# A SwiGLU FFN multiplied as 2x2 blocks with seven block products for eight, in a decoder step on one core

## The chip, the core and the metric

The kernel runs on one core of one Trainium2 chip. A core has TensorE (matmuls, PE in the rows; PEld is its weight load, which overlaps PE), VectorE (DVE), ScalarE (ACT), GpSimd (POOL) and SyncE (SP, which here issues nearly all DMAs). The engines run each their own instruction list and meet at semaphores. The metric is the time of one execution of the program on the device, in microseconds; less is better.

## The reference

One layer of a decoder: RMSNorm, one combined projection, sparse attention (compressed, selected and window branches) beside a pooling group, an output projection with a second norm and the residual, and then the part that the change touches, for 1024 prompt rows and 64 sample rows (1088 rows in all) of width 1024, with 2816 columns in the hidden layer:

```python
D_FF = -(-8 * D_MODEL // (3 * 256)) * 256
...
def ffn_block(x, g_pre, g_post, w_gate, w_up, w_down):
    h = rms_norm(x, g_pre)
    f = (jax.nn.silu(h @ w_gate) * (h @ w_up)) @ w_down
    return x + rms_norm(f, g_post)
```

All values are fp32. The kernel writes each fp32 operand as a high and a low part in fp16 and forms every product from three fp16 matmuls (high-high, high-low, low-high), summed in PSUM.

## The kernel before

Up to about 715 us of the span the program loads, projects and attends. Then come four stages.

**Output projection and second norm.** Nine row tiles t (eight of 128 rows, the last of 64). TensorE forms `project(t)` (L1667: 8 slices of the contraction, 2 halves of 512 columns, 3 matmuls each, so 48) and then `turn(t-1)` (L1678: 8 transposes of the normed rows of the tile before). GpSimd splits the mix operand of a tile ahead of it (`slot_mix`, L1636 and L1640); ScalarE makes the sums of squares (`norms`), VectorE the residual rows x1 (`residual`), the normed rows (`normed`) and, from PSUM, the transposed operand h2 (`save`). ScalarE and VectorE split h2 into its parts (`high`, `low`). The residual rows x1 of all tiles stay in SBUF.

**Gate and up.** For each of 22 tiles f of 128 hidden columns TensorE takes three chunks of rows (384, 384, 320) and for each chunk 24 matmuls with w_gate and 24 with w_up (L1700). Two 512 KB DMAs bring the raw weights of a tile, ScalarE casts the high part (L1791), VectorE makes the low part (L1930). Out of PSUM, ScalarE applies silu (L1819), VectorE multiplies (L1965), ScalarE casts (L1821) and GpSimd makes the low part (L1650).

**Down.** For each of 8 output tiles k TensorE takes the same three chunks, 66 matmuls each over the 22 hidden tiles (L1700 too); the weights (1408 KB each) are split as before (L1795, L1934), ScalarE copies the results out (L1844).

**End.** The last output tile's chunks, transposes back (L1736), the norm's squares (L1864), the scaling (L1994), the adding of x1 (L1653 on GpSimd, L1999 on VectorE) and the stores.

The order on every engine is the order in which the code is written; no scheduler moves anything. Semaphores carry the waits. The free regions of SBUF are laid out by hand in one `arena`.

## Time and profile before

| | us |
|---|---|
| median of 3 runs | 1589.15 (1588.97 to 1590.52) |
| profiled execution, span | 1590.2 |
| TensorE busy | 1446.0 (91%) |
| matmuls of gate and up, first to last | 827.70 to 1317.16 |
| matmuls of down with the transposes among them | 1319.97 to 1567.76 |
| VectorE, ScalarE, GpSimd busy | 709.0, 552.8, 407.0 |

The page shows one execution; times are counted from the start of its span. A row of the chain says when a group of instructions starts and how long it takes, with its engine, line and count. Rows of lines give the busy time of a group, the mean duration of one instruction in ns (for a matmul this holds its whole way through the array, and matmuls overlap), and the idle time before it. The granted clock of TensorE is 1.00 at 2.4 GHz and 0.50 at 1.2 GHz.

### The profile page before, as it was taken

To read this page: it belongs to the slowest core of one execution; us is meant where nothing else is said; L and a number is where in the kernel's file an instruction comes from. 1 tells how busy PE (TensorE), PEld (TensorE's weight loads), DVE (VectorE), ACT (ScalarE), POOL (GpSimd) and SP (SyncE) were. 2 spreads that over 40 slices of the span, in tenths; PEclk is the share of its full clock that TensorE was granted. 3 is DMA by queue.
4 is the path that set the end of the run, shared out by engine and by line. 5 is a ranking of instruction groups with operands and counts; after the bars stand their busy time and mean duration, and the time that the engine had idled before them with its cause. 6 is when DMAs were issued, how large, how long until landed. Compare 5 with 4: busy or idle time off the path is not lost.

```text
span 1590.2 us, 25581 instructions
## 1 busy us (share of the span) xinstructions
PE 1446.0 (91%) x10276; PEld 855.7 (54%) x10276; DVE 709.0 (45%) x1176; ACT 552.8 (35%) x1203; POOL 407.0 (26%) x459
## 2 busy tenths in 40 slices
PE   5498897887899889979979999999999999999996
PEld 3244443544444446644446666666666665666664
DVE  5799995784788536665551111111111120100103
ACT  5233324655677456653341222212222121111103
POOL 1344433785667501013201111111111110000004
PEclk9699998977999899989989999999999999999998
DMA  9666643000000256752111111111111121121102
GB/s 379 217 216 202 208 153 115 1 1 1 1 2 1 107 239 279 310 161 62 53 46 40 53 53 34 45 53 53 53 33 46 53 73 37 47 63 36 36 14 113
DMA packets 93475, 146.59 MB, mean 92 GB/s; under 512 B 3691, under 2 KB 74831, under 8 KB 91143
## 3 DMA queue, kind: packets, MB, share of 16 engines
q1 hardware_dynamic: 81823, 78.43, 15.7%
q0 software_dynamic: 11520, 67.11, 11.7%
q8 instruction: 50, 0.82, 0.2%
q14 instruction: 26, 0.21, 0.0%
q10 hardware_dynamic: 56, 0.01, 0.0%
...
## 4 chain that ended last, share of the span: by engine, by line
PE 61%; ACT 1%; DVE 1%; DMA 1%; issue 1%; POOL 0%; DVEq 0%; POOLq 0%; ACTq 0%
PE psum L1700 46%; PE psum L1667 6%; PE psum L1218 2%; PE psum L1230 2%; PE psum L1256 1%; PE psum L1278 1%; DMA arena<-in_cache_kv_sel,sel_idx 1%; PE psum L807 1%; PE psum L1736 0%; ACT arena L1352 0%; PE psum L1678 0%; DVE arena L1994 0%; ACT arena L1864 0%; PE psum L1285 0%; PE psum L1234 0%
## 5 line engine op out<-in xcount | busy, mean ns | idle before, releaser
L1700 PE MATMUL psum<-arena 128*128 128x384 f16 (+1 forms) x4752 | 734.8, 318 | 5.4 <-POOL arena L1650 2.8
L1700 PEld LDWEIGHTS psum<-arena 128*128 128x128 f16 x4752 | 466.2, 98 | 273.5 <-issue 10.5
L1965 DVE SCALAR_TENSOR_TENSOR arena<-psum,arena 128x384 f32<-128x384 f32 (+1 forms) x66 | 35.4, 536 | 349.1 <-ACT arena L1819 349.1
L1650 POOL TENSOR_TENSOR arena<-arena 128x384 f32 (+1 forms) x66 | 57.7, 874 | 465.2 <-ACT arena L1821 465.2
L2308 PE MATMUL psum<-arena 128*128 128x512 f16 (+1 forms) x768 | 153.2, 360 | 0.0
L1819 ACT ACTIVATE arena<-psum 128x384 f32<-128x384 f32 (+1 forms) x66 | 31.2, 473 | 338.0 <-PE psum L1700 338.0
L1128 POOL TENSOR_TENSOR arena<-arena 128x768 f32<-128x768 f32 (+3 forms) x96 | 131.3, 1382 | 5.0
L997 ACT ACTIVATE arena<-psum,arena 128x384 f32<-128x384 f32 (+3 forms) x192 | 104.7, 554 | 53.3 <-DVE arena L1041 23.0
L2075 POOL DMA_INDIRECT arena<-in_cache_kv_cmp,cmp_idx x64 | 85.3, 1332 | 140.3 <-DVE arena L2239 100.0
L2308 PEld LDWEIGHTS psum<-arena 128*128 128x128 f16 x768 | 76.1, 99 | 72.7 <-issue 4.7
L1934 DVE SCALAR_TENSOR_TENSOR arena<-arena 128x2816 f16<-128x2816 f32 x8 | 24.7, 3093 | 173.7 <-ACT arena L1795 173.7
L1667 PE MATMUL psum<-arena 128*128 128x512 f16 (+1 forms) x432 | 97.3, 387 | 4.9 <-POOL arena L1640 4.9
L941 PE MATMUL psum<-arena 128*128 128x128 f32 x528 | 90.2, 296 | 9.2 <-POOL arena L1128 9.1
L953 PE MATMUL psum<-arena 128*64 128x256 f32 x528 | 90.5, 424 | 3.6 <-DVE arena L1061 2.8
L1038 DVE TENSOR_REDUCE arena<-psum 128x2 f32<-128x768 f32 (+3 forms) x96 | 85.5, 891 | 13.4 <-PE psum L928 10.5
L941 PEld LDWEIGHTS psum<-arena 128*128 128x128 f32 x528 | 59.3, 147 | 53.5 <-issue 37.2
L928 PE MATMUL psum<-arena 64*128 64x384 f16 (+3 forms) x576 | 64.5, 333 | 23.9 <-ACT arena L997 12.5
L1653 POOL TENSOR_TENSOR arena<-arena 128x1024 f32<-128x1024 f32 x7 | 16.3, 2366 | 247.4 <-DVE arena L1994 247.4
L1844 ACT ACTIVATE arena<-psum 128x384 f32 (+3 forms) x21 | 9.9, 473 | 188.2 <-PE psum L1700 188.2
L1930 DVE SCALAR_TENSOR_TENSOR arena<-arena 128x2048 f16<-128x2048 f32 x22 | 50.4, 2293 | 52.3 <-ACT arena L1791 52.3
L2238 DVE TENSOR_TENSOR arena<-arena 128x1024 f32<-128x1024 f32 x56 | 68.3, 1220 | 12.0 <-DMA arena<-in_cache_kv_cmp,cmp_idx 11.1
L1667 PEld LDWEIGHTS psum<-arena 128*128 128x128 f16 (+1 forms) x432 | 43.4, 101 | 55.9 <-POOL arena L1640 5.1
...
## 6 DMA issues: line engine op xcount, KB each, us to landing
arena<-in_w_gate SPq DMA_DIRECT2D x22, 512.0 KB, 3.9
arena<-in_w_up SPq DMA_DIRECT2D x22, 512.0 KB, 5.1
arena<-in_w_down SPq DMA_DIRECT2D x8, 1408.0 KB, 7.0
arena<-in_x_prompt SPq DMA_DIRECT2D x16, 512.0 KB, 4.7
...
arena<-in_cache_kv_win SPq DMA_DIRECT2D x8, 512.0 KB, 3.5
out_y_prompt<-arena SPq DMA_DIRECT2D x8, 512.0 KB, 2.6
...
```

The source lines that it names most:

```text
L928: ins = pe.matmul(bank(2 * (x.n % 2) + g)[:, 0:x.nb * P], qT_half[r, NT - 1 - u.i, qp, x.j, :], kT_half[r, kp, 1 if u.kind == "sel" else 0 ...
L941: ins = pe.transpose(bank(4 + t % 2)[:, (2 * g + jj) * P:(2 * g + jj + 1) * P], u.P[:, jj, g, k * P:(k + 1) * P], ident)
L953: ins = pe.matmul(bank(u.bank)[g * HD:(g + 1) * HD, 0:2 * P], z_all[:, u.k0 + k, u.v0 + g * HD:u.v0 + (g + 1) * HD], pT[t % 3][:, g, :], s ...
L997: ins = nc.scalar.activation(u.P[:, x.jj, g, x.b0 * P:(x.b0 + x.nb) * P], bank(2 * (x.n % 2) + g)[:, 0:x.nb * P], ACT.Exp, bias=neg_m[x.n ...
L1038: ins = nc.vector.tensor_reduce(neg_m[x.n % 4], S, AX, ALU.max, negate=True)
L1128: ins = nc.gpsimd.tensor_tensor(part, part, x[:, c, :].unsqueeze(2).broadcast_to([P, G, nb * P]), ALU.mult)
L1650: nc.gpsimd.tensor_tensor(row(1), silu_out[c][:, 0:c1 - c0], row(0), ALU.subtract).then_inc(act_ready, 1)
L1667: ins = pe.matmul(bank(2 * s + h)[0:n, :], mix_slot[s][xp][:, k, 0:n], w_out[wp][:, k, 512 * h:512 * (h + 1)], start=(k == 0 and i == 0), ...
L1700: ins = pe.matmul(out[:, 0:c1 - c0], w[wp][:, k, :], x[xp][:, k, c0:c1], start=(k == 0 and i == 0), stop=(k == n_k - 1 and i == 2))
L2075: nc.gpsimd.indirect_dma_start(raw[k % RAW].rearrange("p c r -> p (c r)"), None, cmp_rows, bass.IndirectOffsetOnAxis(ap=cmp_idx[:, k:k + 1 ...
L2238: step(nc.vector.tensor_tensor(rows, rows, pos, ALU.mult))
L2308: ins = pe.matmul(dst[:, 0:n], hT[s][xp][:, k, :], w_in[wp][:, k, c0:c0 + n], start=(k == 0 and i == 0), stop=(k == KD - 1 and i == 2))
```

## The change

The FFN's three matrix products are now computed by blocks. The operand h2 is cut into 2 halves of the contraction and 2 halves of the rows (B11, B21 on the left, B12, B22 on the right, 544 rows each), the weights into 2 halves of the contraction and 2 halves of the output (A11 to A22). Seven block products take the place of eight, with sums of blocks as operands: S1 to S4 of the weights, T1 to T4 of h2 and later of the activation. A block product of gate and up has 4 slices of the contraction, 3 matmuls each, in two chunks of 272 rows: 12 matmuls for each product and chunk, 14 of those (168 matmuls) for a unit, which is one pair of hidden tiles (f, f+11) of one of the two matrices. There are 22 units, gate and up in turn. In the down product one of 28 steps s has one operand of 11 slices and two chunks: 66 matmuls of 272 columns. P1, P6, P5 and P3 of a unit add to one another in one PSUM bank for each chunk: each waits until the sum so far has been copied out. P4 adds to P7 in the same way; P2 stands alone.

What else it adds: on GpSimd the sums of h2 (`h_sums`, 4 for a pair of row tiles), of the weights (`w_sum`, 4 for a unit) and of the down weights (`d_sum`, one or two of 1408 columns for a step), and the low halves of the activation's sums (`combine_low`); on ScalarE and VectorE the splits of these sums, copies and adds of single products (`save_u`, `take`, `copy_out`, `add_out`). Row tiles of the output projection are taken in pairs (m, m+4), which lie side by side in the two halves. The rows x1 are written to DRAM as they are made and read back (`x1_dram`) in the last stage. Raw down weights come in 40 DMAs of 704 KB through a ring of 5 buffers. The diff, cut to what bears on the order and on the cost:

```diff
+        OPS = ("B11", "B21", "T1", "T4", "T3", "T2", "B22")
+        HALF, TC = 544, 272
...
+        W_OPS = ("A11", "A22", "A12", "S1", "S2", "S3", "S4")
...
+        PRODUCTS = {"P1": ("A11", "B11"), "P6": ("S2", "T2"), "P2": ("A12", "B21"), "P5": ("S1", "T1"),
+                    "P7": ("S3", "T3"), "P3": ("S4", "B22"), "P4": ("A22", "T4")}
...
+        D_ORDER = ("P1", "P2", "P6", "P5", "P7", "P4", "P3")
+        D_LOADS = {"P1": ((0, 0),), "P2": ((1, 0),), "P6": ((0, 4), (1, 4), (0, 0)), "P5": (), "P7": ((0, 0), (0, 4)), "P4": ((1, 4),),
+                   "P3": ((1, 0), (0, 0))}
...
+        PREP_AT = {s: max(s - 2, -1) for s in range(LAST)}
+        PREP_AT.update({LAST: 21, LAST + 1: 22, LAST + 2: 23, LAST + 3: 24})
...
+        ORDER = [(p, c) for p in ("P6", "P2", "P5", "P7", "P3", "NEXT", "P4") for c in range(2)]
...
+            with sp.Fori(0, KF - 1) as f:
+                sp.wait_ge(w_low, f * 14 + 14)
+                load_gu(f + 1, 0)
+                sp.wait_ge(w_low, f * 14 + 21)
+                load_gu(f + 1, 1)
...
+            for i, (s, kh, m) in enumerate(d_load):
+                if i == 2:
+                    sp.wait_ge(a_low, A0 + 4 * KF)
+                if i >= NR:
+                    sp.wait_ge(dw_low, d_load[i - NR][0] + 1)
+                sp.dma_start(d_raw[i % NR], down_v[:, kh * KF:(kh + 1) * KF, m * P:(m + 1) * P]).then_inc(dl_loaded[i % NR], 16)
...
+                pool.wait_ge(h2_ready, m * 4 + 2)
+                nc.gpsimd.tensor_tensor(b11, b12, b11, ALU.subtract).then_inc(h2_sums, 1)
+                pool.wait_ge(h2_sums, m * 4 + 1)
+                nc.gpsimd.tensor_tensor(b12, b22, b12, ALU.subtract).then_inc(h2_sums, 1)
+                pool.wait_ge(h2_sums, m * 4 + 2)
+                nc.gpsimd.tensor_tensor(b22, b22, b11, ALU.subtract).then_inc(h2_sums, 1)
+                pool.wait_ge(h2_sums, m * 4 + 3)
...
+            with pool.Fori(0, 2) as m:
+                slot_mix(m + 1, 1)
+                h_sums(m)
+                slot_mix(m + 2, 0)
+            slot_mix(3, 1)
+            h_sums(2)
+            slot_mix(NT, 0)
...
+                pool.wait_ge(w_low, u * 7 + 2)
+                nc.gpsimd.tensor_tensor(raw_q["S1"], raw_q["A21"], raw_q["A22"], ALU.add).then_inc(w_sums, 1)
+                pool.wait_ge(w_sums, u * 4 + 1)
+                nc.gpsimd.tensor_tensor(raw_q["S3"], raw_q["A11"], raw_q["A21"], ALU.subtract).then_inc(w_sums, 1)
+                pool.wait_ge(w_sums, u * 4 + 2)
...
+                if name in ("P6", "P7", "P3"):
+                    for i in range(d_first[s], d_first[s + 1]):
+                        pool.wait_ge(dl_loaded[i % NR], 16 * (i // NR + 2))
+                n = d_sums[0]
+                if name == "P6":
+                    nc.gpsimd.tensor_tensor(s1_f[m], raws[0], raws[1], ALU.add).then_inc(dw_sums, 1)
+                    pool.wait_ge(dw_sums, n + 1)
+                    nc.gpsimd.tensor_tensor(raws[2], s1_f[m], raws[2], ALU.subtract).then_inc(dw_sums, 1)
...
-                        ins = pe.matmul(out[:, 0:c1 - c0], w[wp][:, k, :], x[xp][:, k, c0:c1],
-                                        start=(k == 0 and i == 0), stop=(k == n_k - 1 and i == 2))
-                return ins
...
+                        ins = pe.matmul(out[:, 0:TC], w[wp][:, k, :], x[xp][:, k, c * TC:(c + 1) * TC],
+                                        start=(first and k == 0 and i == 0), stop=(k == n_k - 1 and i == 2), skip_group_check=not first)
+                ins.then_inc(done, 1)
...
+                pe.wait_ge(w_low, u * 7 + W_OPS.index(A) + 1)
+                if p == "P1":
+                    if not first:
+                        pe.wait_ge(c12_taken, u * 2 + (c - 3))
+                elif p == "P6":
+                    pe.wait_ge(s1_saved, u * 2 + (c + 1))
+                elif p == "P5":
+                    pe.wait_ge(chain_saved, saved_at(u, "P6", c))
+                elif p == "P3":
+                    pe.wait_ge(chain_saved, saved_at(u, "P5", c))
+                elif p == "P4":
+                    pe.wait_ge(c22_taken, u * 2 + (c + 1))
...
+            w_highs(0, 0, W_OPS)
             step.at(end)
             norms(NT, 0)
...
+            high_right(3)
+            high_sums(3)
...
+            act.wait_ge(p1_done, 1)
+            save_1(0, 0, 0)
+            save_u(0, 0, "P6", 0)
+            save_u(0, 0, "P5", 0)
+            silu_12(0, 0)
+            high_left(4)
+            high_right(4)
+            high_sums(4)
...
+                step.at(start + (m * 2) * 3)
+                residual(m * 2 + 2, 0, m * 16 + 32, m * 16 + 16)
+                save(m * 2 + 1, 1)
+                normed(m * 2 + 2, 0)
+                low_right(m)
+                step.at(start + (m * 2 + 1) * 3)
+                residual(m * 2 + 3, 1, m * 16 + 32, m * 16 + 16)
+                low_sums(m)
+                dve.wait_ge(h2_ready, m * 4 + 4)
+                save(m * 2 + 2, 0)
+                normed(m * 2 + 3, 1)
+                low_left(m + 1)
...
+            w_lows(0, 0, W_OPS)
+            residual(NT, 0, 16 * (NT // 2 + 1), 16 * (NT // 2))
             save(NT - 1, 1)
             normed(NT, 0)
-            low(NT - 1, 1)
+            low_right(3)
...
```

`PRODUCTS` gives for each product its weight block and its right operand; `ORDER` is the order of a unit, where NEXT is P1 of the next unit. Three places of the instruction lists follow, each before and now.

TensorE, from the last tile of the output projection into the FFN (L1667 and L1927 project, L1678 and L1938 turn, L1959 a block product):

```order
L1667 MATMUL psum<-arena 64x512 [waits x1_done,mix_ready]
L1667 MATMUL psum<-arena 64x512 x47
L1678 MATMUL psum<-arena 128x128 [waits h2_read,xn_ready]
L1678 MATMUL psum<-arena 128x128 x7
L1678 MATMUL psum<-arena 128x64 [waits h2_read,xn_ready]
L1678 MATMUL psum<-arena 128x64 x7
L1706 UNCONDITIONAL_BRANCH [waits h2_ready]
L1706 ISA
L1711 ISA [waits gu_split]
```

```order
L1927 MATMUL psum<-arena 64x512 [waits x1_done,mix_ready]
L1927 MATMUL psum<-arena 64x512 x47
L1938 MATMUL psum<-arena 128x128 [waits h2_read,xn_ready]
L1938 MATMUL psum<-arena 128x128 x7
L1959 MATMUL psum<-arena 128x272 [waits w_low,x1_done,h2_ready]
L1959 MATMUL psum<-arena 128x272 x11
L1959 MATMUL psum<-arena 128x272 [waits w_low]
L1959 MATMUL psum<-arena 128x272 x11
L1959 MATMUL psum<-arena 128x272 [waits s1_saved,w_low]
L1959 MATMUL psum<-arena 128x272 x11
L1959 MATMUL psum<-arena 128x272 [waits w_low]
L1959 MATMUL psum<-arena 128x272 x11
```

The transposes of the 64-row tile (128x64 before) no longer stand ahead of the FFN's first matmuls: P1 and P2 of the first chunk come first, then P6 with a wait for `s1_saved`, ScalarE's copy of P1.

ScalarE at the same place (L1770/L1771 and L2092/L2093 the norms, L1787 and L2117 to L2126 high parts of h2, L1791 and L2135 high parts of weights, L1819 silu, L2164 the copy of P1, L2169 of later sums):

```order
L1791 ACTIVATE arena<-arena 128x2048 [waits gu_loaded]
L1770 ACTIVATE arena<-psum 64x1024 [waits o_done]
L1771 ACTIVATE arena<-arena 64x1 [waits act_norm_step]
L1770 ACTIVATE arena<-arena 64x1024 [waits x1_done]
L1771 ACTIVATE arena<-arena 64x1 [waits act_norm_step]
L1787 ACTIVATE arena<-arena 128x8x128 [waits h2_read]
L1787 ACTIVATE arena<-arena 128x8x64 [waits h2_read]
L1791 ACTIVATE arena<-arena 128x2048 [waits gu_loaded,h2_ready]
L1819 ACT_TABLE_LOAD [waits act_ready]
L1819 ACTIVATE arena<-psum 128x384 [waits gu_done]
```

```order
L2135 ACTIVATE arena<-arena 128x512 [waits weight_loaded5]
L2135 ACTIVATE arena<-arena 128x512 x2
L2135 ACTIVATE arena<-arena 128x512 [waits w_sums] x4
L2092 ACTIVATE arena<-psum 64x1024 [waits o_done]
L2093 ACTIVATE arena<-arena 64x1 [waits act_norm_step]
L2092 ACTIVATE arena<-arena 64x1024 [waits x1_done]
L2093 ACTIVATE arena<-arena 64x1 [waits act_norm_step]
L2117 ACTIVATE arena<-arena 128x4x128 [waits h2_read]
L2125 ACTIVATE arena<-arena 128x8x128 [waits h2_sums]
L2126 ACTIVATE arena<-arena 128x8x128
L2164 ACTIVATE arena<-psum 128x272 [waits p1_done]
L2169 ACTIVATE arena<-psum 128x272 [waits prod_done] x2
```

Seven splits of the first unit's weights, four of them behind `w_sums`, now stand ahead of the norms of the last tile, and the high parts of h2's sums, behind `h2_sums`, ahead of the copy of P1.

GpSimd at the end of the output projection (L1636/L1640 and L1798/L1802 are `slot_mix`, L1815 to L1821 `h_sums`, L1838 to L1842 `w_sum`):

```order
L1636 ISA [waits o_done]
L1636 COPY arena<-arena 128x1024
L1640 TENSOR_TENSOR arena<-arena 128x1024 [waits mix_high]
L1635 REGISTER_ALU
L1636 ISA [waits o_done]
L1636 COPY arena<-arena 128x1024
L1640 TENSOR_TENSOR arena<-arena 128x1024 [waits mix_high]
L1624 REGISTER_ALU
L1624 COMPARE_AND_BRANCH
L1636 CAST arena<-arena 128x8x64 [waits o_done]
L1640 TENSOR_TENSOR arena<-arena 128x8x64 [waits mix_high]
```

```order
L1826 COMPARE_AND_BRANCH
L1798 CAST arena<-arena 128x1024 [waits o_done]
L1802 TENSOR_TENSOR arena<-arena 128x1024 [waits mix_high]
L1815 TENSOR_TENSOR arena<-arena 128x512 [waits h2_ready]
L1817 TENSOR_TENSOR arena<-arena 128x512 [waits h2_sums]
L1819 TENSOR_TENSOR arena<-arena 128x512 [waits h2_sums]
L1821 TENSOR_TENSOR arena<-arena 128x512 [waits h2_sums]
L1798 CAST arena<-arena 128x8x64 [waits o_done]
L1802 TENSOR_TENSOR arena<-arena 128x8x64 [waits mix_high]
L1838 TENSOR_TENSOR arena<-arena 128x512 [waits w_low]
L1840 TENSOR_TENSOR arena<-arena 128x512 [waits w_sums]
L1842 TENSOR_TENSOR arena<-arena 128x512 [waits w_sums]
```

Four sums of h2, the first behind `h2_ready`, now stand between the mix operands of an odd tile and of the next even tile; the same happens in each turn of the loop before these rows. The first unit's weight sums follow.

## Rows read from the trace of the kernel before

**Rows 1.** The page, busy time of each engine and share of the span.

```profile
PE 1446.0 (91%) x10276; PEld 855.7 (54%) x10276; DVE 709.0 (45%) x1176; ACT 552.8 (35%) x1203; POOL 407.0 (26%) x459
```

**Rows 2.** Chain that ended last: start us, us, engine, tile, line, count.

```profile
806.82 10.49 PE psum L1667 x48
...
827.70 489.46 PE psum L1700 x3168
...
1319.97 236.21 PE psum L1700 x1518
1556.18 2.62 PE psum L1736 x24
1558.80 8.96 PE psum L1700 x66
```

**Rows 3.** TensorE by line and shape: busy us, mean ns, idle before.

```profile
L1700 PE MATMUL psum<-arena 128*128 128x384 f16 x3168 | 524.0, 328 | 5.4 <-POOL arena L1650 2.8 <-DVE arena L1925 2.5
L1700 PE MATMUL psum<-arena 128*128 128x320 f16 x1584 | 220.1, 299 | 0.0
...
L466 PE MATMUL psum<-arena 128*128 128x64 f16 x96 | 3.5, 193 | 1.2 <-ACT arena L559 1.2
```

**Rows 4.** Timeline of TensorE in the input projection (L2308).

```profile
122.68 10.52 PE L2308 MATMUL psum<-arena 128*128 128x512 f16 x48
...
135.22 8.20 PE L2308 MATMUL psum<-arena 128*128 128x512 f16 x48
```

**Rows 5.** Timeline of the output projection, all engines.

```profile
712.02 2.87 POOL L1640 TENSOR_TENSOR arena<-arena 128x1024 f16<-128x1024 f16 x1 [0.19 <-POOL arena L1636]
...
749.96 1.04 POOL L1636 CAST arena<-arena 128x1024 f16 x1 [7.88 <-PE psum L1667]
750.49 10.52 PE L1667 MATMUL psum<-arena 128*128 128x512 f16 x48
751.18 2.13 POOL L1640 TENSOR_TENSOR arena<-arena 128x1024 f16<-128x1024 f16 x1 [0.18 <-POOL arena L1636]
...
756.23 0.75 DVE L1913 TENSOR_SCALAR arena<-arena 128x1024 f32 x1
...
795.58 1.16 POOL L1640 TENSOR_TENSOR arena<-arena 128x512 f16<-128x512 f32 x1 [0.18 <-POOL arena L1636]
```

**Rows 6.** Windows: us, PE, PEld, DVE, ACT, POOL busy, clock, DMA.

```profile
825.00:830.00 5.00, 2.47 (x10) 1.13 (x9) 2.26 (x4) 3.22 (x3) 0.00 (x0) 0.50 0.02 3
830.00:835.00 5.00, 5.00 (x23) 2.60 (x22) 1.63 (x1) 0.60 (x1) 0.00 (x0) 0.69 0.39 115
1320.00:1325.00 5.00, 5.00 (x21) 2.55 (x22) 2.69 (x1) 2.27 (x1) 0.00 (x0) 0.66 0.00 0
```

**Rows 7.** The other engines by line and shape, columns as Rows 3.

```profile
L1930 DVE SCALAR_TENSOR_TENSOR arena<-arena 128x2048 f16<-128x2048 f32 x22 | 50.4, 2293 | 52.3 <-ACT arena L1791 52.3
L1934 DVE SCALAR_TENSOR_TENSOR arena<-arena 128x2816 f16<-128x2816 f32 x8 | 24.7, 3093 | 173.7 <-ACT arena L1795 173.7
L1965 DVE SCALAR_TENSOR_TENSOR arena<-psum,arena 128x384 f32<-128x384 f32 x44 | 24.5, 558 | 219.1 <-ACT arena L1819 219.1
...
L1821 ACT ACTIVATE arena<-arena 128x384 f32 x40 | 20.9, 522 | 28.9 <-DVE arena L1965 28.9
L1795 ACT ACTIVATE arena<-arena 128x2816 f16<-128x2816 f32 x8 | 20.4, 2544 | 1.1 <-POOL arena L1650 1.1
...
L1128 POOL TENSOR_TENSOR arena<-arena 128x512 f32<-128x512 f32 x28 | 31.1, 1111 | 0.6
...
L1653 POOL TENSOR_TENSOR arena<-arena 128x1024 f32<-128x1024 f32 x7 | 16.3, 2366 | 247.4 <-DVE arena L1994 247.4
```

**Rows 8.** DMA issues: count, KB each, median us to landing.

```profile
arena<-in_w_up SPq DMA_DIRECT2D x22, 512.0 KB, 5.1
arena<-in_w_down SPq DMA_DIRECT2D x8, 1408.0 KB, 7.0
```

**Rows 9.** Timeline after the last matmul, VectorE scaling a group.

```profile
1572.65 3.67 DVE L1994 SCALAR_TENSOR_TENSOR arena<-psum,arena 128x1024 f32<-128x1024 f32 x3
```

899 lines of the change are left out of this document (660 added, 239 removed).

## The prediction

> **What bounds the kernel now.** I read the busy line of the page first: TensorE is busy for 91% of the span and no other engine for half of it [rows 1]. Then the chain of what ended last: after 806.82 it is TensorE nearly throughout, 3168 matmuls of gate and up in 489.46 us, then 236.21, 2.62 and 8.96 us for down with its transposes [rows 2]. The list by line and shape says that TensorE idled only 5.4 us before all 4752 of them [rows 3]. So the FFN stands at the array's own rate, and what counts is how many columns stream and who is late once fewer do.
>
> The rate: 48 matmuls of 512 columns take 10.52 us, of which some 0.16 is the drain of the last, so 215.8 ns each, 213.3 ns of streaming at 2.4 GHz and 2.5 more. In the row of 8.20 us the code has 24 matmuls of 512 columns and 24 of 280 (the rows of a project with two outputs); without the drain and the 24 long ones 2.86 us are left, 119.2 ns each, again 2.5 above 280 columns [rows 4]. So 272 columns cost 115.8 ns, and a product of 12 matmuls 1.39 us. The weight load is no floor: 96 matmuls of 64 columns, each with its own 128x128 load, were busy 3.5 us, 36 ns each [rows 3].
>
> The Trainium skill speaks against this size: "TensorE: Matmul & The Clock Gate", section "Back-to-back issue gap", has a stream of load and matmul pairs at about 81 ns for 128 columns, some 25 ns above streaming. By that (an estimate from the page) the new FFN would be 5544 x 22 ns = 122 us dearer than mine, and slower than before, as a rival below has it. The row of 280 columns shows no such surcharge.
>
> **The change part by part.** Arithmetic alone: before, 3168 matmuls of 384 columns at 162.5 ns and 1584 of 320 at 135.8 give 729.9 us; after, 22 x 168 + 28 x 66 = 5544 of 272 columns give 642.0. That is 87.9 us less. Where it goes I work out in four stretches of time against the profiled execution (span 1590.2; the median of the runs is 1.05 lower).
>
> *Output projection, +21.* TensorE has 11.2 us for a tile (10.4 for 48 matmuls, 0.9 for the transposes). GpSimd now does `h_sums` between the mix operands of an odd tile and the next even one. These sums wait for `low_right`, which stands on VectorE behind `normed` of the even tile. In the old trace that tile's project ended at about 749.7 (the cast at 749.96 answers to it) and its normed rows at 756.98 [rows 5]. Half a tile's low part takes 0.7 more (1024/2 elements at the 1.1 ns of L1934 [rows 7] and an access): 757.7. Four sums of 512 elements at 1.11 to 1.16 us [rows 5, 7] with 0.18 between: 763.0. Then the next mix operand, 1.04 + 0.18 + 2.13 + 0.1: 766.5. TensorE, which began the odd tile at 750.49, would want it at 761.7. It waits 4.8 to 4.9 us, and so for tiles 4, 6 and 8; behind the mix operand nothing else stands but the next one, in time. Such a gap also lowers the clock: after an idle of 2.8 us the granted clock was 0.66 over 1320 to 1325, after the one before 827.70 it was 0.50, then 0.69 over 830 to 835 [rows 3, 6]. At half the clock these cost 1.5 and 2.7 us; I take 2.1 for each gap of this size or larger. Sum 3 x (4.9 + 2.1) = 21.0; the bounds are 0 (all in time) and 3 x 9. On VectorE and ScalarE the added splits (about 3 us for a pair of tiles) lie in the 22 us that the pair takes.
>
> *From the start of the last project to the first down matmul, -43.* Before: 806.82 to 1319.97, 513.2 us [rows 2]. After, counted from the last project's start: ScalarE reaches `w_highs` at 6.3 (norms of tile 7 until 0.5, two high parts of sums, the save of tile 6 behind their low parts at 5.2, one more high part); A11 and A22 are split at 8.8 on VectorE; four sums of the weights (4 x 1.34) end at 14.2 and the seventh high part at 14.9. Only then come the norms of the last tile, though its project ended at 10.4. Start of norm to normed rows is 7.1 (749.9 to 756.98 [rows 5]): 22.0. Low part 22.7, `h_sums(3)` 28.0, two high parts of 1024 (1.04 each) 30.2, and only behind these, on ScalarE, the copy of P1: 30.6. TensorE has done P1 and P2 by 14.1, and P6 waits 16.6 us. The change lets FFN work begin before the last transposes, but the wait takes that back. Then five products, 2.7 for the low clock, 0.6 for the step from P5's copy to P3: 41.0. Transposes 41.9. The right columns of the 64-row tile (save, splits, four small sums, splits) take until 48.2, 6.3 us idle. Nine more products with the low clock and a step: 64.0. By now 16 of the 308 products are done; 292 x 1.39 = 405.8 follow, so down begins at 469.8. The old 2.8 us wait before down goes, since a first step's weights and operand are ready while P4 of the last unit runs. 469.8 - 513.2 = -43.4; were the first unit free of waits, it would be -75.
>
> That the steady units keep pace is the claim on which most rests. A unit has 19.45 us. For two units VectorE has 14 low parts of 512 elements (0.6, from L1930 and L1934), 12 takes of 272 columns (0.45, from L1965) and some 5 us more: 19 of 38.9 us; ScalarE 14 high parts (0.6), 14 copies and silus of 272 (0.4) and 7 of 544 (0.65): 19; GpSimd 8 sums (1.16) and 4 low parts (1.2): 15 [rows 7]. The chain P6, P5, P3 has four other products between, 4.2 to 5.6 us, for a copy that needs 0.6. The tightest place is the reload of the one raw weight buffer. The last weight split of an up unit stands behind two casts of the activation and ends near 19.2; the load lands about 6 us later (5.1 and the issue [rows 8]); two splits, two takes and a silu later ScalarE copies P5's first chunk at 9.9 of the next unit, where P3 wants it at 11.1. Slack about 1 us, then 2 us at the copy of P1.
>
> *Down, -16.* Before: 1319.97 to 1567.76, 247.8 [rows 2]. After: 1848 x 115.8 = 214.0 and six tiles' transposes 5.2. A step takes 7.64. Steps 8 to 11 (P6) need three raw loads each in a ring of five, and the last load of a step waits until the step before it has its low part. So the steps' weights form a serial loop: load 5.0 (between 512 KB at 5.1 and 1408 KB at 7.0, a lone one somewhat quicker [rows 8]), two GpSimd sums of 1408 elements at 3.0 (from L1128 and L1653), high part 1.36 (L1795 halved and a little), low part 1.63 (L1934), handovers 0.5: 14.7 a step. Step 8's low part is ready at 50.2 after down's start (after step 5, at 45.8), the next at 64.9, 79.6 and 94.3. TensorE wants them at 61.1, 68.7, 76.4 and then 7.64 after. It waits 3.2 and 7.1, and 2.1 for the clock: 12.4. P7 and P3 have two loads a step and come in time. VectorE with two combines a step is busy 7.2 of 7.64, and its low parts have 9 us of slack. 231.6 - 247.8 = -16.2; bounds -28 (no wait) and -5 (sums at 3.3, loads at 5.5, the later steps late too).
>
> *End, -5.* Before, 22.4 us from the last matmul to the end, in which VectorE scaled two groups of tiles, 3.67 each [rows 2, 9]. After, tiles 0 to 5 are turned among the last eight products, and one group is left: add 0.5, copy 0.6, transposes to 3.7, squares and root to 6.3, scaling 3.9, adds 2.5, store as before 4.7: 17.5. Bounds 14 and 22. x1's way through DRAM is queued while the last steps run and costs nothing; without that cover it would be 4.2 MB, some 21 us at the rate of 1408 KB in 7.0 [rows 8].
>
> Sum: 21.0 - 43.4 - 16.2 - 5.0 = -43.6, span 1546.6, time 1546.
>
> **The rivals.** *The waits are covered (0.2).* If GpSimd's sums go faster or overlap more than read here, the gaps of the output projection and of P6 close: 1546 - 21 - 12 = 1513. For it: GpSimd is busy only 407 us. Against: the order is strict, and each sum waits for the one before.
>
> *The units run longer than TensorE's share (0.11): slower than before.* The place is the reload round of the raw weight buffer above. It becomes the bound once the round passes 19.45; the change turns slower from 44/22 = 2 us over that. Casts and sums on GpSimd beside VectorE splits took 2.87 in place of 2.13 us [rows 5], a factor of 1.35; on all sums and low parts of a round (5.4 and 9 us) this is 5 us, of which idle time would take some 2. At 22.5 us a unit: 1546 + 22 x 3 = 1612. Against: both engines are idle half of the time, and a round by itself is about 15 us (load 6, sums 5.4, four splits at its ends).
> The Trainium skill, "SBUF — State Buffer", on the engine side of the ports, has VectorE and GpSimd share one pair, the loser blocked for the whole instruction; by that this factor would be larger for the f32 sums. The row of 2.87 shows some of it.
>
> *The short matmuls cost more than 115.8 ns (0.03),* by waits at every twelfth: 8 ns more each is 44 us and no gain, 1590; 16 ns more are 1635. Against: 2.5 ns at 280 as at 512 columns [rows 4]. The surcharge of the Trainium skill's section named above would come out here.
>
> *Some units stall by the 1 us slack (0.06):* ten pairs with 1 to 2 us, 1556 to 1566, still faster.
>
> **How the numbers follow.** The forecast has 0.6: 1546, its own range 1530 to 1562. The range for 8 in 10 reaches to the covered case and to the stalling units: 1508 to 1580. A change of 0.2% (3 us) is about what a measurement of this kernel can tell from none. Faster: 0.6 + 0.2 + 0.06, less a little for errors that add: 0.85. Slower: 0.12. Same: 0.03.
>
> **What would show it.** Right: 5544 matmuls with 115 to 117 ns spacing; three gaps of 4 to 6 us ahead of projects of even tiles, each after GpSimd; a gap of 15 us or more before the first P6, behind ScalarE; two waits in down at steps 10 and 11; units of 19.4 to 19.6 us. Wrong: units above 20 us, or a spacing above 120 ns, or no gaps before the FFN. The forecast fails most likely in the first unit and in GpSimd's durations.

## The result, and the profile after

The changed kernel takes 1600.9 us (median of 6 runs, 1597.5 to 1603.9) against 1590.0 for the kernel before on the same chip (6 runs): ratio 1.0065, 95% interval 1.0049 to 1.0081. It is slower by 11 us; 1546 us was forecast, and the range ended at 1580.

| stretch | before | after | change | forecast |
|---|---|---|---|---|
| to the start of the last project | 806.8 | 821.0 | +14.2 | +21.0 |
| from there to the first down matmul | 513.2 | 474.0 | -39.1 | -43.4 |
| down | 247.8 | 284.1 | **+36.3** | **-16.2** |
| end | 22.4 | 16.9 | -5.5 | -5.0 |
| span | 1590.2 | 1596.0 | +5.8 | -43.6 |

Three stretches came within 7 us. Down is off by 52 us. The table is of one profiled execution, whose span lies 3 us under the median of the six. The first down matmul stands inside a merged row and is reckoned back from its steps, so down and end are good to 0.3 us. The busy line of the page, answering to [rows 1]:

```profile
PE 1380.2 (86%) x11068; PEld 938.7 (59%) x11068; DVE 1017.4 (64%) x1623; ACT 666.0 (42%) x1491; POOL 675.7 (42%) x598
```

TensorE is busy for 66 us less, VectorE for 308 more and GpSimd for 269 more. The average does not say where that hurts. TensorE's timeline does (start, us, engine, line, count, and in brackets the idle time before and who ended it). Output projection and first unit:

```profile
765.48 12.22 PE L1927 MATMUL psum<-arena 128*128 128x512 f16 x48 [4.15 <-POOL arena L1802]
...
793.95 12.18 PE L1927 MATMUL psum<-arena 128*128 128x512 f16 x48 [4.14 <-POOL arena L1802]
...
820.99 12.23 PE L1927 MATMUL psum<-arena 128*64 128x512 f16 x48 [2.75 <-POOL arena L1802]
...
853.96 6.66 PE L1959 MATMUL psum<-arena 128*128 128x272 f16 x36 [16.93 <-ACT arena L2164]
...
870.10 9.90 PE L1959 MATMUL psum<-arena 128*128 128x272 f16 x60 [5.33 <-DVE arena L2371]
```

The three gaps ahead of even tiles are there, each behind GpSimd's mix operand, and each project after one takes 1.7 us longer than the 10.52 of the others. P6 of the first chunk waits 16.9 us for ScalarE's copy of P1 (16.6 forecast).

The steady units, one window of 40 us (columns: TensorE, its weight loads, VectorE, ScalarE, GpSimd busy with their counts, granted clock, DMA share and GB/s):

```profile
1100.00:1140.00 40.00, 39.89 (x345) 33.48 (x343) 22.58 (x35) 17.00 (x39) 17.33 (x13) 1.00 0.19 52
```

That is 116 ns for each matmul, with 0.1 us of idle; three more such windows have 344 to 347 matmuls and at most 0.3 us of idle. Now down (L2494 is VectorE's split of a weight block into its low part, L2522 the low part of a combined activation block):

```profile
1269.95 94.00 PE L1959 MATMUL psum<-arena 128*128 128x272 f16 x810 [0.34 <-ACT arena L2169]
1364.25 7.82 PE L1959 MATMUL psum<-arena 128*128 128x272 f16 x66 [0.31 <-DVE arena L2494]
1378.54 10.67 PE L1959 MATMUL psum<-arena 128*128 128x272 f16 x66 [6.47 <-DVE arena L2494]
1393.45 17.70 PE L1959 MATMUL psum<-arena 128*128 128x272 f16 x132 [4.24 <-DVE arena L2494]
1411.41 7.82 PE L1959 MATMUL psum<-arena 128*128 128x272 f16 x66 [0.26 <-DVE arena L2494]
1420.67 7.82 PE L1959 MATMUL psum<-arena 128*128 128x272 f16 x66 [1.45 <-DVE arena L2494]
1432.21 9.46 PE L1959 MATMUL psum<-arena 128*128 128x272 f16 x66 [3.72 <-DVE arena L2494]
...
1476.12 7.82 PE L1959 MATMUL psum<-arena 128*128 128x272 f16 x66 [1.45 <-DVE arena L2494]
...
1536.64 6.32 PE L1959 MATMUL psum<-arena 128*128 128x272 f16 x33 [9.51 <-DVE arena L2522]
```

Nine steps run at 7.64 us, from 1295.0 (nine steps before the end of the first row) to 1363.95. Steps 10 and 11 wait 6.5 and 4.2; the loop of P6 was forecast to make them wait 3.2 and 7.1. But then nearly every step waits for VectorE's low part: the steps start 9.27 us apart, and 11.55 where GpSimd makes the weight sums of P7 while VectorE splits the weights of steps 15 to 18. All waits of down for L2494 are 36.0 us in 14 places, and the one for the combined operand B22 (L2522) is 9.5. The longer waits also lower the clock: after 3.72 us of wait step 15 took 9.46 in place of 7.82, with a granted clock of 0.55 from 1432.3 to 1436.0; after 1.45 us step 14 took 7.82, at 1.00 from 1420.7 to 1428.0.

I call a slot what an engine does for one step, and a combination the making of one slice of a combined activation block: VectorE adds high parts (L2515) and then the low parts that GpSimd's `combine_low` has added (L2517), ScalarE takes the new high part (L2283), VectorE the new low part (L2522). One slot of 9.27 us, all engines but TensorE:

```profile
1403.27 0.78 DVE L2509 TENSOR_TENSOR arena<-psum,arena 128x272 f32<-128x272 f32 x2
...
1403.96 0.71 DVE L2515 TENSOR_TENSOR arena<-arena 128x544 f32<-128x544 f16 x1
1404.71 0.72 DVE L2517 TENSOR_TENSOR arena<-arena 128x544 f32<-128x544 f32 x1
1405.36 0.72 DVE L2515 TENSOR_TENSOR arena<-arena 128x544 f32<-128x544 f16 x1
1405.47 0.66 ACT L2283 ACTIVATE arena<-arena 128x544 f16<-128x544 f32 x1 [5.05 <-DVE arena L2517]
1405.52 1.63 POOL L1902 TENSOR_TENSOR arena<-arena 128x544 f32<-128x544 f16 x1 [5.82 <-DVE arena L2517]
1406.11 1.62 DVE L2517 TENSOR_TENSOR arena<-arena 128x544 f32<-128x544 f32 x1
1407.77 0.66 ACT L2283 ACTIVATE arena<-arena 128x544 f16<-128x544 f32 x1 [1.64 <-DVE arena L2517]
1407.81 1.22 POOL L1902 TENSOR_TENSOR arena<-arena 128x544 f32<-128x544 f16 x1 [0.66 <-DVE arena L2517]
1408.33 1.36 ACT L2265 ACTIVATE arena<-arena 128x1408 f16<-128x1408 f32 x1
1409.72 1.63 DVE L2494 SCALAR_TENSOR_TENSOR arena<-arena 128x1408 f16<-128x1408 f32 x1 [1.99 <-ACT arena L2265]
1411.27 1.35 DVE L2522 TENSOR_TENSOR arena<-arena 128x544 f16<-128x544 f32 x2
```

Two things make 6.4 us of work last 9.3. The second L2517 takes 1.62 us where the first took 0.72: GpSimd's `combine_low` had started 0.59 before it, and it ends 0.6 after that has ended. (`combine_low` is stretched too: 1.63 beside VectorE's L2515, 1.22 at 1407.81, where VectorE stands idle.) And VectorE stands idle for 1.99, since ScalarE takes the two combinations first and the weight split (L2265), which had been free to start, last. Where a weight sum of P7 falls into the slot a third thing comes on top:

```profile
1427.52 3.15 POOL L1886 TENSOR_TENSOR arena<-arena 128x1408 f32<-128x1408 f32 x1
1428.26 3.90 DVE L2494 SCALAR_TENSOR_TENSOR arena<-arena 128x1408 f16<-128x1408 f32 x1 [1.99 <-ACT arena L2265]
```

The split started 0.74 after GpSimd's weight sum and ended 1.49 after it, so it had moved hardly anything while the sum ran: 3.90 for 1.63. GpSimd's two sums for each step of P3 do the same later, ahead of the waits of 3.7 and 3.6 at steps 22 and 23 and of the 9.5 for B22:

```profile
1502.24 3.90 DVE L2494 SCALAR_TENSOR_TENSOR arena<-arena 128x1408 f16<-128x1408 f32 x1 [1.99 <-ACT arena L2265]
...
1516.73 7.02 DVE L2494 SCALAR_TENSOR_TENSOR arena<-arena 128x1408 f16<-128x1408 f32 x2 [1.99 <-ACT arena L2265]
```

### The profile page after: what moved, and what is told of

It reads as the page before. It is cut to its first block, busy times and chain, and to the rows that moved or that the text cites. A ratio compares the mean times of both kernels' runs of the same rounds, so it can differ in the third digit from the quotient of the medians.

```text
span 1596.0 us, 28892 instructions
## 1 busy us (share of the span) xinstructions
PE 1380.2 (86%) x11068; PEld 938.7 (59%) x11068; DVE 1017.4 (64%) x1623; ACT 666.0 (42%) x1491; POOL 675.7 (42%) x598
## 4 chain that ended last, share of the span: by engine, by line
PE 16%; DVE 15%; issue 12%; DMA 10%; ACT 7%; POOL 3%; DVEq 1%; SPq 1%; ACTq 0%; POOLq 0%
PE psum L1959 6%; DMA arena<-in_w_up 3%; DMA arena<-in_w_gate 3%; DVE arena L2376 3%; PE psum L1927 2%; ACT arena L2135 2%; DMA arena<-in_cache_kv_sel,sel_idx 2%; DVE arena L2418 2%; DVE arena L2494 2%; PE psum L1221 2%; ACT arena L2265 2%; PE psum L1233 2%; DVE arena L2517 1%; DVE arena L2522 1%; DVE arena L2515 1%
## 5 line engine op out<-in xcount | busy, mean ns | idle before, releaser
L1959 PE MATMUL psum<-arena 128*128 128x272 f16 x5544 | 666.7, 284 | 70.3 <-DVE arena L2494 36.0
L1959 PEld LDWEIGHTS psum<-arena 128*128 128x128 f16 x5544 | 549.2, 99 | 186.5 <-DVE arena L2494 40.1
L2376 DVE SCALAR_TENSOR_TENSOR arena<-arena 128x512 f16<-128x512 f32 x154 | 138.4, 929 | 171.4 <-ACT arena L2135 171.4
L2879 PE MATMUL psum<-arena 128*128 128x512 f16 (+1 forms) x768 | 153.0, 360 | 0.0
L2494 DVE SCALAR_TENSOR_TENSOR arena<-arena 128x1408 f16<-128x1408 f32 x28 | 64.9, 2319 | 88.5 <-ACT arena L2265 88.5
L2879 PEld LDWEIGHTS psum<-arena 128*128 128x128 f16 x768 | 76.2, 99 | 72.6 <-issue 4.3
L1927 PE MATMUL psum<-arena 128*128 128x512 f16 (+1 forms) x432 | 101.7, 398 | 16.1 <-POOL arena L1802 15.9
L2135 ACT ACTIVATE arena<-arena 128x512 f16<-128x512 f32 x154 | 89.4, 624 | 44.5 <-DMA arena<-in_w_up 28.7
L1851 POOL TENSOR_TENSOR arena<-arena 128x544 f32 (+1 forms) x44 | 60.1, 1375 | 90.5 <-ACT arena L2184 90.5
L1838 POOL TENSOR_TENSOR arena<-arena 128x512 f32<-128x512 f32 x22 | 28.7, 1306 | 162.2 <-DVE arena L2376 162.2
L944 PEld LDWEIGHTS psum<-arena 128*128 128x128 f32 x528 | 58.8, 146 | 53.1 <-issue 36.3
L1902 POOL TENSOR_TENSOR arena<-arena 128x544 f32<-128x544 f16 x33 | 46.3, 1405 | 95.0 <-DVE arena L2517 94.9
L1927 PEld LDWEIGHTS psum<-arena 128*128 128x128 f16 (+1 forms) x432 | 44.2, 103 | 71.0 <-POOL arena L1802 16.8
L1355 ACT ACTIVATE arena<-psum 128x512 f32<-128x512 f32 (+2 forms) x104 | 53.1, 558 | 59.0 <-PE psum L1221 38.6
## 6 DMA issues: line engine op xcount, KB each, us to landing
arena<-x_dram SPq DMA_DIRECT2D x2, 2048.0 KB, 10.8
```

The source lines that it names most:

```text
L944: ins = pe.transpose(bank(4 + t % 2)[:, (2 * g + jj) * P:(2 * g + jj + 1) * P], u.P[:, jj, g, k * P:(k + 1) * P], ident)
L1927: ins = pe.matmul(bank(2 * s + h)[0:n, :], mix_slot[s][xp][:, k, 0:n], w_out[wp][:, k, 512 * h:512 * (h + 1)], start=(k == 0 and i == 0), ...
L1959: ins = pe.matmul(out[:, 0:TC], w[wp][:, k, :], x[xp][:, k, c * TC:(c + 1) * TC], start=(first and k == 0 and i == 0), stop=(k == n_k - 1 ...
L2135: nc.scalar.activation(slots[w][name][0], raw_q[name], ACT.Copy, scale=WS).then_inc(w_high, 1)
L2376: nc.vector.scalar_tensor_tensor(slots[w][name][1], raw_q[name], WS, slots[w][name][0], ALU.mult, ALU.subtract).then_inc(w_low, 1)
L2494: nc.vector.scalar_tensor_tensor(d_slot(s)[1], d_operand(s), WS, d_slot(s)[0], ALU.mult, ALU.subtract).then_inc(dw_low, 1)
```

## The experiments

Theory A: down is paced by VectorE's slot, which is longer than TensorE's step for three reasons (the order on ScalarE, `combine_low`, the weight sums). Rival B: the way of the weights (loads, ring, sums) paces it. Beside it stand two smaller questions: whether the gaps of the output projection and of the first unit come from the order alone. Each kernel is the changed one with the edit shown. e1 and e3 leave out work that the result needs, the others don't. Times are medians, ratios are against the kernel before. "Down" runs from its first matmul to the end of its last, to 0.3 us, in each profile.

| run | us | ratio, 95% | down |
|---|---|---|---|
| changed kernel | 1600.9 | 1.0049 to 1.0081 | 284.4 |
| e1_no_combines | 1545.7 | 0.9698 to 0.9739 | 232.0 |
| e2_high_first | 1586.0 | 0.9968 to 0.9990 | 268.5 |
| e3_small_sum | 1592.6 | 1.0008 to 1.0036 | 275.2 |
| e5_p6_ring | 1592.4 | 0.9994 to 1.0031 | 275.4 |
| e4_mix_first | 1593.5 | 1.0008 to 1.0031 | 284.8 |
| e6_first_unit | 1593.9 | 1.0000 to 1.0031 | 282.3 |
| e7_vector_sum | 1597.0 | 1.0022 to 1.0052 | 281.6 |
| e8_all | 1559.1 | 0.9777 to 0.9822 | 259.4 |
| e9_vector_sums | 1536.4 | 0.9632 to 0.9671 | 236.0 |
| e10_vector_only | 1524.9 | 0.9570 to 0.9602 | 229.1 |

The stretch before the output projection, the same in all, varied: it ended between 714.2 and 722.4 us. So stretches are compared by their length.

**e1_no_combines.**

```diff
+        combine_due = {slot: [] for slot in range(28)}
...
-                elif s % 4 == 0 and B in combine_end:
-                    pe.wait_ge(mid_low, combine_end[B])
...
-            sp.wait_ge(mid_low, combine_end["B22"])
+            sp.wait_ge(down_done, 40)
```

> Leaves out every combination of activation blocks in the down projection (combine_low, combine_start, combine_high, combine_end_); the products that would use them read the plain blocks, and the residual reload waits for the end of P7 instead. All matmuls, loads, weight sums and copies stay. Theory A (the down stage is paced by VectorE's slot, which is longer than TensorE's 7.64 us from step 12 on): without them VectorE has 3.2 us of work a slot, the steps from 12 on go back to 7.64 us, the waits before step 10 and 11 (the weight loop of P6) stay or shrink a little; down projection 284.1 -> 235 to 245 us, whole kernel 40 to 48 us less than the changed kernel, about 1553 to 1561. Rival B (the weights' way, raw loads and GpSimd's sums, paces the stage): at most 10 us less, 1590 or more.

1545.7 us, 55 less, and down 52 shorter. TensorE's longest waits for another in the last 400 us (line waited for, us in total, times, longest):

```profile
PE psum L1960 <- DVE arena L2492: 9.6, 2, 8.1
```

What is left are the two waits at steps 10 and 11 and 1.4 us at the end; loads and weight sums are all there. So B is out as what paces the stage; its share is P6's loop. The gain was larger than expected, and the 9.5 us for B22, which went too, were not in what I expected.

**e2_high_first.**

```diff
-                for x in combine_due[slot]:
-                    combine_high(*x)
                 for s in prep_due.get(slot, ()):
                     d_high(s)
+                for x in combine_due[slot]:
+                    combine_high(*x)
```

> One order changed: on ScalarE each slot of the down projection splits the next weight block (d_high) before it takes the activation combinations (combine_high). Theory A: the 2.0 us in which VectorE waits in each slot from 10 on (0.66 + 1.36 on ScalarE) go, the slot falls from 9.27 to about 7.64 where GpSimd's combine_low still holds VectorE for 0.9, down projection 12 to 20 us shorter, whole kernel 1581 to 1589. Rival (VectorE's time is all work and port contention, its waits merely move behind the next instruction): under 5 us.

1586.0, down 16 shorter: the order on ScalarE cost 15 us. The split now follows without idle. The slot falls to 8.2 us, though, not to 7.64, and beside P7's sums it is still 11.2; there the trace shows the time in another place:

```profile
1428.65 1.61 DVE L2494 SCALAR_TENSOR_TENSOR arena<-arena 128x1408 f16<-128x1408 f32 x1
...
1428.81 2.53 POOL L1902 TENSOR_TENSOR arena<-arena 128x544 f32<-128x544 f16 x1 [0.66 <-DVE arena L2517]
1430.19 5.34 DVE L2522 TENSOR_TENSOR arena<-arena 128x544 f16<-128x544 f32 x2
...
1431.30 3.64 POOL L1886 TENSOR_TENSOR arena<-arena 128x1408 f32<-128x1408 f32 x1
```

The split is back at 1.61. Now it is GpSimd's `combine_low` that takes 2.53 for 1.22, and the two L2522, 1.35 us by themselves, take 5.34 around `combine_low` and the weight sum. In these rows whoever comes second waits, on either engine.

**e3_small_sum.**

```diff
-                    nc.gpsimd.tensor_tensor(raws[0], raws[0], raws[1], ALU.subtract).then_inc(dw_sums, 1)
+                    nc.gpsimd.tensor_tensor(raws[0][:, 0:1, :], raws[0][:, 0:1, :], raws[1][:, 0:1, :], ALU.subtract).then_inc(dw_sums, 1)
```

> GpSimd's four weight sums of P7 are cut to one of eleven slices (the instruction and its increments stay, its length falls from 3.15 us to about 0.3; the product's weights are thereby wrong in ten slices). Theory A (a GpSimd instruction that overlaps VectorE's d_low blocks it for its whole length): d_low at P7 1.63 us in place of 3.90, the P7 slots 9.3 us in place of 11.55, down projection 7 to 10 us shorter, whole kernel about 1591 to 1594. Rival (d_low is late because the sum itself is late in a serial chain load -> sum -> high -> low): also some microseconds shorter, but then d_low's own duration would have been 1.63 already; the length of d_low tells the two apart.

8 us less, down 9.2 less, as expected:

```profile
1438.45 0.46 POOL L1886 TENSOR_TENSOR arena<-arena 128x128 f32<-128x128 f32 x1
1439.19 1.62 DVE L2494 SCALAR_TENSOR_TENSOR arena<-arena 128x1408 f16<-128x1408 f32 x1 [1.99 <-ACT arena L2265]
```

The split starts 0.74 after the sum's start, as before, and takes 1.62 where it took 3.90; the steps there are 9.27 us apart. So its length came from the sum beside it, not from a late chain.

**e5_p6_ring.**

```diff
-                    sp.wait_ge(dw_low, d_load[i - NR][0] + 1)
+                    s0 = d_load[i - NR][0]
+                    if D_ORDER[s0 // 4] == "P6" and i - NR < d_first[s0] + 2:
+                        sp.wait_ge(dw_sums, 2 * (s0 % 4) + 1)
+                    else:
+                        sp.wait_ge(dw_low, s0 + 1)
```

> Two of the three raw weight buffers of each P6 step are given back to the loads after GpSimd's first sum, not after VectorE's split. Theory: the serial loop of 14.3 us per P6 step (load 4.6, sums 3.17 + 3.17, high 1.39, low 1.64) opens, and the waits before steps 10 and 11 (6.5 and 4.2 us, with the slow clock behind each) fall to 0 to 2 us each; down projection 8 to 13 us shorter, whole kernel 1588 to 1593. Rival: VectorE's slots, slower than TensorE's from slot 10 on, decide the end in any case and are fed by GpSimd, so the gain is given back at steps 12 and after: under 3 us.

8.5 us less, down 9.0 less. The waits before steps 10 and 11 are 3.3 (0 to 2 were expected) and 0.2 us in place of 6.5 and 4.2; what follows is unchanged at 9.27 and 11.55:

```profile
1382.55 9.44 PE L1963 MATMUL psum<-arena 128*128 128x272 f16 x66 [3.34 <-DVE arena L2498]
1392.18 7.82 PE L1963 MATMUL psum<-arena 128*128 128x272 f16 x66 [0.19 <-DVE arena L2498]
```

So the loop of P6 adds to VectorE's slots and isn't hidden by them. The rival (under 3 us) is out.

**e4_mix_first.**

```diff
                 slot_mix(m + 1, 1)
-                h_sums(m)
                 slot_mix(m + 2, 0)
+                h_sums(m)
             slot_mix(3, 1)
-            h_sums(2)
             slot_mix(NT, 0)
+            h_sums(2)
```

> On GpSimd the mix operand of the next tile (slot_mix) goes ahead of the four activation sums (h_sums) in the output projection; nothing else changes. Theory (the 4.15, 4.14 and 2.75 us that TensorE waits for slot_mix, and the 1.7 us that each following project loses to the lower clock, are all due to the place of h_sums): the three waits go and the projects that followed them take 10.5 us again, so last project start at 805 to 808 us in place of 821.0, whole kernel 12 to 16 us shorter, 1585 to 1589. Rival (the sums, now late, hold the chain of ScalarE's copies and the waits reappear at P1 of the first unit or in VectorE's saves): under 6 us.

Only 7.4 us less. From the first project to down's start it is 571.3 us in place of 580.1. The three gaps are gone, but others stand in their stead (the second row is the first unit's):

```profile
777.68 1.66 PE L1938 MATMUL psum<-arena 128*128 128x128 f32 x8 [4.14 <-DVE arena L2345]
...
850.21 5.75 PE L1959 MATMUL psum<-arena 128*128 128x272 f16 x36 [19.32 <-ACT arena L2164]
```

The wait for P1's copy grew from 16.9 to 19.3, and transposes now wait 4.1 for VectorE, which is again stretched beside a GpSimd instruction:

```profile
774.93 2.70 DVE L2345 TENSOR_SCALAR arena<-arena 128x1024 f32<-128x1024 f32 x1
774.95 2.13 POOL L1802 TENSOR_TENSOR arena<-arena 128x1024 f16<-128x1024 f16 x1 [0.19 <-POOL arena L1798]
```

Alone L2345 takes 0.75. The 7.4 us lie between what the theory (12 to 16) and the rival (under 6) had; the gaps come from the order, but other waits are close behind them.

**e6_first_unit.** ScalarE (VectorE's low parts are divided in the same way):

```diff
-            w_highs(0, 0, W_OPS)
+            w_highs(0, 0, W_OPS[0:3])
             step.at(end)
             norms(NT, 0)
             high_right(3)
-            high_sums(3)
+            w_highs(0, 0, W_OPS[3:7])
...
             save_1(0, 0, 0)
+            high_sums(3)
```

> In the first unit ScalarE copies P1 out before it takes the sums of the fourth pair of tiles, and splits of the weights S1 to S4 go behind the 64-row tile's norm, on ScalarE and VectorE. Theory (P6 of the first chunk waits 16.9 us only because that copy is queued behind high_sums, which wait for GpSimd): the wait falls to 3 to 8 us, whole kernel 6 to 13 us shorter, 1588 to 1595. Rival (what is moved behind is needed as soon for the next products): the stall moves to a product of the second chunk or of unit 1 and the time changes by under 3 us.

7.0 us less, as the theory had it; first project to down's start 572.2 us. The wait of 16.9 became 5.16 and 4.32:

```profile
847.71 4.26 PE L1959 MATMUL psum<-arena 128*128 128x272 f16 x24 [5.16 <-ACT arena L2164]
...
856.29 1.98 PE L1959 MATMUL psum<-arena 128*128 128x272 f16 x12 [4.32 <-ACT arena L2169]
```

**e7_vector_sum.** GpSimd's sum of P7 goes; on VectorE, ahead of the combinations:

```diff
+                        nc.vector.tensor_tensor(r0, r0, r1, ALU.subtract).then_inc(dw_sums, 1)
```

> The four weight sums of P7 (3.15 us each on GpSimd) are done by VectorE, ahead of its combinations. Theory (in those slots a GpSimd sum costs VectorE 2.3 us of blocking, 3.90 for 1.63, and an own sum of 1408 elements costs about 1.6): d_low at P7 back to 1.63 us, the P7 slots 10.6 to 11.0 us in place of 11.55, whole kernel 2 to 5 us shorter, 1596 to 1599, although VectorE now has more work. Rival (VectorE is bound by its own work alone, blocking is small): the slots become 12.5 to 13 and the kernel 4 to 6 us longer.

4 us less, down 2.8 less, although VectorE got four instructions of 1.61 us more. The split that stood beside P7's sum takes 1.63 again, and the steps there are 10.8 us apart (the next split starts at 1453.35):

```profile
1442.55 1.63 DVE L2493 SCALAR_TENSOR_TENSOR arena<-arena 128x1408 f16<-128x1408 f32 x1 [1.99 <-ACT arena L2264]
...
1446.07 1.61 DVE L2532 TENSOR_TENSOR arena<-arena 128x1408 f32<-128x1408 f32 x1
```

**e8_all.** The edits of e2, e4, e5, e6 and e7, and a table (for more than two in a slot, VectorE starts and ends them in pairs):

```diff
-        COMBINE_AT = {"T3": (2, 2, 1, 1, 1, 1, 1, 1, 1), "T4": (0,) * 6 + (1, 1, 1, 2, 2, 2, 2), "B22": (0,) * 13 + (2, 2, 2, 2, 2, 1)}
+        COMBINE_AT = {"T3": (4, 3, 1, 1, 1, 1), "T4": (0,) * 6 + (2, 2, 2, 2, 1, 1, 1), "B22": (0,) * 13 + (1, 2, 2, 2, 2, 2)}
```

> All of it together: mix operand first, first unit reordered, P6 ring released early, ScalarE's weight split ahead of the combinations, P7's sums on VectorE, and a table of the combinations that puts 7 of T3 in slots 4 and 5 (where VectorE has no sums of products to take yet) and only one a slot in the slots of P7's sums. Theory (three separate losses, in output projection, first unit and VectorE's slots): output projection -14, first unit -6 to -12, down projection 284 -> 242 to 252 us, whole kernel 1536 to 1552, some 40 to 50 us under the kernel before. Rival (the losses hide one another, or GpSimd and VectorE contend as much wherever the work lies): 1560 or more.

1559.1: 32 us under the kernel before of the same runs, but 7 above the expected range. First project to down's start is 563.3, 16.8 less: the 8.8 of e4 and 7.9 of e6 add up. Down, at 259.4, fell short by 7. VectorE's slots with P7's sums are 7.0 us apart now, but between the splits of steps 7 and 8 lie 17 us, and TensorE waits 5.6 there:

```profile
1339.23 3.57 DVE L2522 TENSOR_TENSOR arena<-arena 128x544 f32<-128x544 f32 x1
1342.30 3.52 POOL L1887 TENSOR_TENSOR arena<-arena 128x1408 f32<-128x1408 f32 x1
1342.72 4.57 DVE L2499 SCALAR_TENSOR_TENSOR arena<-arena 128x1408 f16<-128x1408 f32 x1
```

My table had pushed the combinations into GpSimd's sums for P6, with the same stretching; and likewise at the sums of P3 (waits of 4.6 and 12.0).

**e9_vector_sums.** As e8 with all weight sums on VectorE, another table, and the load of `g_post_ffn` ahead of the residual's (not shown here):

```diff
+                for s in prep_due.get(slot, ()):
+                    d_sum(s)
...
+        COMBINE_AT = {"T3": (2, 2, 1, 1, 1, 1, 2, 1), "T4": (0,) * 7 + (1, 2, 2, 2, 2, 2), "B22": (0,) * 13 + (1, 2, 2, 2, 2, 2)}
```

> As the combined kernel (1559.1 us), with three edits in the down projection: all weight sums (P6, P7, P3) on VectorE, so that GpSimd has the 33 combine_low alone; a table of the combinations with two a slot at most; g_post_ffn's load ahead of the residual's. Theory (a GpSimd sum of 3.15 us that meets VectorE costs it the whole overlap, a VectorE sum costs 1.6): the 17 us between the splits of steps 7 and 8 and the 19 us between those of steps 24 and 25 shrink to 8 to 12, no DVE instruction of combine or split over 2.7 us, and the 4.2 us that TensorE waited for the first scaled tile go; down projection 259.4 -> 242 to 252 us, whole kernel 1542 to 1553. Rival (VectorE's own work is now the bound and grows by 12 sums): 1556 to 1570.

1536.4, down 236.0, both 6 us better than the expected range. Down's waits above 0.7 us are 3.6, 3.8 and 3.7, all near its end; that for the first scaled tile went from 4.2 to 0.6. Three edits were made at once, so their shares of the 23 us are not separated.

**e10_vector_only.** As e9, without `combine_low` on GpSimd:

```diff
-                nc.gpsimd.tensor_tensor(y, acts[x2][1][:, k, :], acts[x1_][1][:, k, :], op).then_inc(mid_lo, 1)
+                nc.vector.tensor_tensor(mid_f[i % 2][1], acts[x2][1][:, k, :], acts[x1_][1][:, k, :], op).then_inc(mid_lo, 1)
```

> As the one before, and the 33 combine_low (1.63 us each on GpSimd) are done by VectorE as well (0.72 us each by its other additions of 544), so that GpSimd does nothing in the down projection until the last residual additions. Theory (what GpSimd does beside VectorE is paid for by VectorE in blocking, about 0.9 us a combine_low, so taking it over at 0.72 costs nothing): within 6 us of the one before, on either side. Rival (GpSimd's work is done beside VectorE's and is free): 33 x 0.72 = 24 us more VectorE work, of which 15 us or more show in the time.

1524.9 us, ratio to before 0.957 to 0.960: 65 us under the kernel before and 76 under the changed one. Down is 6.9 us shorter than in e9. (3.3 of the 10.2 us between the two spans lie in stretches that are alike in both.) Taking work away from an engine that is mostly idle in down and giving it to the one that paces the stage made the kernel faster. VectorE by line between 1290 and 1500 (busy us, mean ns), e9:

```profile
L2474 DVE SCALAR_TENSOR_TENSOR arena<-arena 128x1408 f16<-128x1408 f32 x26 | 43.1, 1661 | 21.6 <-ACT arena L2244 21.3
L2502 DVE TENSOR_TENSOR arena<-arena 128x544 f16<-128x544 f32 x33 | 37.8, 1178 | 0.0
L2497 DVE TENSOR_TENSOR arena<-arena 128x544 f32<-128x544 f32 x33 | 35.6, 1077 | 1.1
```

and e10, with 33 more instructions (L2484):

```profile
L2463 DVE SCALAR_TENSOR_TENSOR arena<-arena 128x1408 f16<-128x1408 f32 x26 | 42.1, 1621 | 20.5 <-ACT arena L2233 20.5
L2487 DVE TENSOR_TENSOR arena<-arena 128x544 f32<-128x544 f32 x33 | 23.9, 725 | 1.1
...
L2484 DVE TENSOR_TENSOR arena<-arena 128x544 f32<-128x544 f16 x33 | 23.7, 718 | 0.0
L2492 DVE TENSOR_TENSOR arena<-arena 128x544 f16<-128x544 f32 x33 | 22.5, 718 | 0.0
```

GpSimd's 33 instructions lengthened VectorE's by 33 x (0.460 + 0.352) + 26 x 0.040 = 27.8 us; doing them itself costs VectorE 23.7. Of the two `combine_low` in a slot the first stretches an L2497 (0.72 -> 1.62), the second the pair of L2502 (1.35 -> 2.37). I had expected the two kernels within 6 us of each other; the medians are 11.5 apart, the stage 6.9. VectorE's balance accounts for 4.1 of that, and what made the rest is open.

## Why the prediction was wrong

- **TensorE's rate** held: 116 ns for a matmul of 272 columns in the windows of the units (115.8 forecast), so the 87.9 us of arithmetic are real, and the rival of dearer short matmuls is out. The Trainium skill ("TensorE: Matmul & The Clock Gate", section "Back-to-back issue gap") gives about 81 ns for 128 columns in a stream of loads and matmuls, where its formula for a single matmul gives about 56; those 25 ns, carried over to 272 columns, are not in the windows of the units. The same passage gives about 131 ns for 512 columns, where rows 4 have 215.8 ns; the measurement decides.
- **Output projection**, +14.2 for +21.0: the place, the number and the cause of the gaps were right. Sizes: 4.15, 4.14 and 2.75 for 4.9 each, and 1.7 of clock for 2.1; the third 1.7 falls behind the start of the last project, into the next stretch.
- **First unit**, -39.1 for -43.4: the waits of 16.9 and 5.3 stood where they were forecast (16.6 and 6.3). From 880.58 to 1295.0 a matmul took 116.7 ns with its small waits, 3 us more in all than at 115.8.
- **Units**: the slack of 1 us in the reload round held; a unit took 19.6 us. So none of the signs by which the forecast would have shown itself wrong (units above 20 us, a spacing above 120 ns, no gaps before the FFN) came, and it was wrong all the same. The rival that GpSimd and VectorE stretch one another was priced in the units, where both are idle half of the time, and given 0.11. Its mechanism came true in down, where I had not looked for it.
- **Down** is the step that failed, in one sentence of it: "VectorE with two combines a step is busy 7.2 of 7.64, and its low parts have 9 us of slack." Its own work was even less, 6.4 (9.27 less 1.99 of idle and 0.9 of stretching). But I added up durations of one engine and called the rest slack, without following the order of the slot over three engines. ScalarE takes the combinations ahead of the split (15 us, e2). `combine_low` and GpSimd's weight sums hold VectorE up (9.2 us of down for those of P7 alone, e3). And the 9 us of slack were not there from step 9 on: P6's loop had made the low parts just in time already, and from step 14 on a slot that was 1.6 to 3.9 us too long went into a wait nearly each time. Without the combinations (e1) down takes 232.0, and the forecast, which had them covered, had 231.6.
- **P6's loop**: 10.7 us of waits for 10.3, and e5, which took most of it away, gained 8.5 us of time. That the sums agree is partly luck: a round took 14.3 us, the last 14.9, for 14.7 (the forecast's own terms add up to 14.5), but the first low part of P6 was ready 54.9 us after down's start, not 50.2, behind sums that took 3.67 and 4.43 us beside VectorE where later ones took 3.16. With the clock steps 10 to 12 lost some 16 us for 12.4.
- **End**: -5.5 for -5.0.

The forecast's bound for down was -5, with "the later steps late too" as one way to it; a chain of 14 waits, of which P6's loop makes only two, was not in it. The sign of the whole hangs on that one stage: 52 us of error against a forecast gain of 44.

On the mechanism the Trainium skill, "SBUF — State Buffer", section "Who interferes with whom", says that a VectorE instruction with both inputs in SBUF contends with GpSimd's reads and that the second to issue blocks until the first has finished. The traces agree: 3.90 for 1.63 with the sum first, 2.53 for 1.22 on GpSimd with the split first. Each ended 0.14 us sooner than if nothing of it had run beside the other. The forecast quoted the rule, but took a factor of 1.35 from one row [rows 5]. If the second waits for the first to end, what it costs is the overlap, not a factor.
